# Eleven weight-panel subtractions of a four-layer transformer kernel, moved from VectorE to GpSimd

## The chip, the cores and the metric

The kernel runs on one core of a Trainium2 chip, as one launch. The metric is the device time of that core in microseconds, the median of the runs. The profile gives the span from the first to the last instruction of one execution.

## The reference, cut to what matters

One sequence of 256 tokens, 1024 wide, goes through four layers, all in float32: two of a first kind (four mixers: HGRN2, GLA, MLA, gated delta net, then a gated feed-forward) and two of a second kind. This case is about the second kind:

```python
def hybrid_layer(x, p_i, ...):
    h = rmsnorm(x, g_pre_mix)
    proj = h @ w_in                        # 1024 -> 3404 columns, split in 16 parts
    # a: index scores choose 64 keys of 256 per query, then attention on them
    o_a = dsa_attention(rope(a_q), rope(a_k), a_v, rope(a_iq), rope(a_ik), iw)
    o_b = forgetting_attention(b_q, b_k, b_v, log_sigmoid(b_f + b_forget))
    o_c = differential_attention(rope(c_q), rope(c_k), c_v, lam, ...)
    o_d = sliding_window_sink_attention(rope(d_q), rope(d_k), d_v, sinks)
    x = x + rmsnorm(concat(o_a, o_b, o_c, o_d) @ w_out, g_post_mix)
    m = square(relu(rmsnorm(x, g_pre_mlp) @ w_up)) @ w_down
    x = x + rmsnorm(m, g_post_mlp)
    return x + sigmoid(x @ w_ple_gate) * (p_i @ w_ple_proj)
```

## The kernel before, in words

The 256 tokens are two tiles of 128. The state `x` stays in SBUF, and so do the activations; only weights are streamed. A weight panel is 128 partitions by 2048 float32 values (256 columns of a 1024-row matrix, 1 MB). Panels go through a ring of eight slots, in a fixed list, loaded by SyncE's queue; SyncE waits for the slot to be given back before it issues a load. Layers are named 10, 11 (first kind) and 20, 21 (second kind).

**Split products.** Most matrix products are made in three passes. A float32 matrix is split into a high part, rounded to the format `fp32r`, and a low part, the rest; TensorE then multiplies high by high, high by low and low by high (`mm3`). A panel is split in two steps. ScalarE copies it, rounded, into a second ring slot (`round_weights`, L2577; it increments `rounded`). VectorE then subtracts that copy from the panel in place (`subtract_rounded`, L2760), which gives the low part, and increments `subtracted`. Before it uses a panel TensorE waits until `subtracted` has reached that panel's number (`split_panel`). Both semaphores count the panels of all layers in the order of the list. TensorE alone gives a panel's two slots back.

**A second-kind layer up to its output projection.** Of the fifteen panels of `w_in`, the first four (in3, in4, in5, in9: the index queries, keys and weights, the forget gate) aren't split. The eleven others, here called panels 1 to 11, are, in the order in10, in11, in6, in7, in12, in0, in1, in8, in2, in13, in14; all are 128 x 2048. Four panels of `w_out` follow as 12 to 15. `PANELS` lists these fifteen.

**The order of work.** Every engine runs its instructions in the order in which the program wrote them. Within this part of the layer that order is written by hand: `ORDER` has a list for TensorE, ScalarE and VectorE, and `emit` takes the next piece of the generator that each word names. The word `panel` is one rounding in ScalarE's list and one subtraction in VectorE's; `in` is a projection's piece (TensorE), its copy out of PSUM (ScalarE), its rotation (VectorE: L2797 multiplies the rotated half from PSUM, L2802 the plain half, L2804 adds); `h` is the split of the layer's input; `index` weighs the index scores (L2927, L2929), `select` picks the 64 largest by rounds of `max` and `match_replace` (L2861 to L2870); `a` to `d` are the mixers: masked scores (L2822) and their maximum (L2826), probabilities (L2846 to L2852), later pieces.

**The split of h** (`split_h_in`, L411 to L420) is done for each token tile: two subtractions of 128 x 512, L417 and L419, and then the semaphore `h_split`. It writes over `h`, so it waits until TensorE has made the small unsplit projection of that tile. TensorE waits for both tiles' `h_split` before its first split panel.

**Between engines.** TensorE needs a free PSUM bank for every product (eight banks, given back by the engine that reads them). The masked scores of mixer c take all eight. The transposes of probabilities (L2242) wait for VectorE's `probs`.

GpSimd has no program of its own.

Of the kernel before, what the change touches and what calls it, by code (L numbers as in the profile page):

```python
# [11 lines left out]
ALU = mybir.AluOpType  # L12
# [8 lines left out]
DEPTH = 2  # L21
# [153 lines left out]
class LayerRing:  # L175
# [27 lines left out]
    def rounded_by_act(self, name):  # L203
        return self.ring.rounded, self.ring.split[f"{self.layer}.{name}"] + 1

    def subtracted_by_dve(self, name):
        return self.ring.subtracted, self.ring.split[f"{self.layer}.{name}"] + 1


# [5 lines left out]
class Memory:  # L215
# [12 lines left out]
    def rounded(self, ap):  # L228
        return bass.AP(tensor=self.other[ap.tensor.name], offset=ap.offset, ap=ap.ap)


def as_float32(ap):
    return ap.bitcast(F32)
# [75 lines left out]
class Kit:  # L309
# [156 lines left out]

    def split_panel(self, pe, ring, name):

        pe.wait_ge(*ring.subtracted_by_dve(name))
        return self.rounded(ring.view(name + "_hi")), self.rounded(ring.view(name))  # L470

    def free_panel(self, ring, name):
# [1646 lines left out]
def block2(nc, ctx, kit, banks, ring_all, A, earlier):  # L2119

    rounded, hT, mixT, x = kit.rounded, kit.hT, kit.mixT, kit.x
# [61 lines left out]
    def scores_of(buffer, t, maps):  # L2183
# [35 lines left out]
            c in panel in c b panel c panel b in c panel in forget b c:2 in b c b:2 a panel b in a:2 panel in split a:4  # L2219
            in d p split:2 d a early panel early d:2 early late d:2 early rest d rest d late rest:2"""),  # L2220
        "DVE": in_order("""
            in:2 panel h panel h in:3 panel:3 in:3 index select index panel in panel c:2 select forget:2 c:2 panel
            forget in b in c panel b c in c panel c in panel b:2 c a c b:2 in b panel a panel a b in a split panel in
            a:3 split:2 d in d:2 panel d early p early d a early rest early d:2 rest late rest late d rest"""),
    }
    MIXERS = [(name, t) for name, *_ in ATTENDED for t in range(NT)]
    maxima, probabilities, exponentials = (turns_in(ORDER[engine], {(name, t): (name, first + t) for name, t in MIXERS})
# [518 lines left out]
    def upper_half_in(act, layer, t):  # L2746
        kit.upper_half_of_hT(act, psum_of(layer), "hT0", t, par_of(layer)("pre_mix"))
        kit.round_upper_half(act, t)

    def vector(dve, layer):  # L2750

        psum, ring, due = psum_of(layer), ring_of(layer), due_in(layer)
# [15 lines left out]
            V.tensor_tensor(rounded(lo), a, as_float32(rounded(hi)), ALU.subtract)  # L2768

        def split_panels():  # L2770
            for name in PANELS:
                subtract_rounded(name)
                yield

# [322 lines left out]

    out = Group()
    out.tensor, out.scalar, out.vector, out.load = tensor, scalar, vector, load
    out.transposes_in, out.upper_half_in, out.lower_half_in = transposes_in, upper_half_in, lower_half_in  # L3100
    out.finish_scalar, out.finish_vector = finish_scalar, finish_vector
    out.angles_of, out.rope_tables, out.columns_in = angles_of, rope_tables, small_in
# [6 lines left out]
def two_blocks(nc, A, out):  # L3109

    with ExitStack() as ctx:
# [27 lines left out]
        with nc.Block() as block:  # L3139
# [38 lines left out]
            def _(act):  # L3178
# [7 lines left out]
                for n, (kind, layer) in enumerate(layers):  # L3186
# [18 lines left out]
                    else:  # L3205
                        for _ in ending:
                            pass

            @block.vector
            def _(dve):  # L3210
                dve.wait_ge(ident_in, 16)
                for t in range(NT):
                    kit.scale_rows(dve, 0, t)
                dve.wait_ge(first.columns_in, 16)
                for t in range(NT):
                    first.lower_half_in(dve, 0, t)
                for n, (kind, layer) in enumerate(layers):
                    if (kind, layer) == (first, DEPTH - 1):
                        kind.vector(dve, layer, second.angles_of)
                    else:  # L3220
                        kind.vector(dve, layer)
                    last = n + 1 == len(layers)
                    for _ in kind.finish_vector(dve, layer, 0):
                        pass
                    if not last:
                        after, its = layers[n + 1]
                        kit.scale_rows(dve, 2 * n + 2, 0)
                    ending = kind.finish_vector(dve, layer, 1)
                    next(ending)
                    if not last:  # L3230
                        if after is second and not its:
                            dve.wait_ge(second.columns_in, 16)
                        after.lower_half_in(dve, its, 0)
                    next(ending, None)
                    if not last:
                        kit.scale_rows(dve, 2 * n + 2, 1)
                        after.lower_half_in(dve, its, 1)
# [25 lines left out]
```

## Time and profile before

| What | us |
|---|---|
| median of three runs | 1697.64 |
| lowest and highest | 1693.14, 1698.69 |
| the profiled execution | 1691.87 |
| its span, first to last instruction | 1689.8 |
| TensorE busy | 1594.9 (94%) |
| VectorE busy | 1093.3 (65%) |
| ScalarE busy | 776.6 (46%) |
| GpSimd busy | 0.2 |

The mean granted clock of TensorE is 0.973 of full speed. PE is TensorE's matmuls, PEld its weight loads, DVE is VectorE, ACT ScalarE, POOL GpSimd, SP SyncE; a name with q is an engine's sequencer (a drain or semaphore instruction). L2760 is line 2760 of the kernel. A busy TensorE isn't TensorE at its peak, since matmuls are pipelined and the clock can be granted at half speed. The span was taken on one execution; the idle time of an engine that bounds nothing costs nothing.

### The profile page before, as it was taken

To read this page: it belongs to the slowest core of one execution; us is meant where nothing else is said; L and a number is where in the kernel's file an instruction comes from. 1 tells how busy PE (TensorE), PEld (TensorE's weight loads), DVE (VectorE), ACT (ScalarE), POOL (GpSimd) and SP (SyncE) were. 2 spreads that over 40 slices of the span, in tenths; PEclk is the share of its full clock that TensorE was granted. 3 is DMA by queue.
4 is the path that set the end of the run, shared out by engine and by line. 5 is a ranking of instruction groups with operands and counts; after the bars stand their busy time and mean duration, and the time that the engine had idled before them with its cause. 6 is when DMAs were issued, how large, how long until landed. Compare 5 with 4: busy or idle time off the path is not lost.

```text
span 1689.8 us, 29634 instructions
## 1 busy us (share of the span) xinstructions
PE 1594.9 (94%) x12124; PEld 1425.8 (84%) x12124; DVE 1093.3 (65%) x1609; ACT 776.6 (46%) x1199; POOL 0.2 (0%) x4
## 2 busy tenths in 40 slices
PE   7998988999999989799999989999999979999998
PEld 7987568998898856799989877899889977799887
DVE  3866666776476665577754898666453798666545
ACT  4534254444435332544444455755344346655434
POOL 0000000000000000000000000000000000000000
PEclk9999898999999989899999999999999989999999
DMA  7521033555642200366554433455554432356552
GB/s 247 157 74 52 1 98 118 190 177 202 192 138 68 77 26 7 114 219 198 189 200 120 125 78 104 145 177 203 188 194 133 136 89 100 125 157 205 182 192 100
DMA packets 186310, 232.23 MB, mean 137 GB/s; under 512 B 22560, under 2 KB 161600, under 8 KB 186048
## 3 DMA queue, kind: packets, MB, share of 16 engines
q1 hardware_dynamic: 186176, 230.34, 42.2%
q8 instruction: 96, 1.57, 0.4%
q14 instruction: 38, 0.31, 0.1%
HBM read 229.28 MB, written 1.05 MB: 136 GB/s over the span
## 4 chain that ended last, share of the span: by engine, by line
PE 81%; DVE 10%; ACT 3%; DVEq 3%; issue 2%; DMA 1%; ACTq 0%; SPq 0%
PE banks L435 80%; DVE all_ring_rounded L2760 2%; DVE all_rest L2929 1%; DVE all_work L2864 1%; DMA all_ring<-in_w_ple_gate 1%; DVEq L2863 1%; ACT all_rest L345 1%; DVE all_work L2848 1%; DVE all_ring_rounded L1612 0%; DVE all_work L2826 0%; PE banks L930 0%; DVE all_work L2822 0%; PE banks L2242 0%; DVE x_state L384 0%; ACT all_rest L2581 0%
## 5 line engine op out<-in xcount | busy, mean ns | idle before, releaser
L435 PE MATMUL banks<-all_mix_rounded,all_ring_rounded 128*128 128x256 f32 (+2 forms) x3584 | 670.4, 288 | 20.6 <-DVEq L431 10.9
L435 PEld LDWEIGHTS banks<-all_mix_rounded,all_ring_rounded 128*128 128x128 f32 (+2 forms) x3584 | 569.6, 194 | 30.0 <-DVEq L431 11.9
L435 PE MATMUL banks<-all_work_rounded,all_ring_rounded 128*128 128x256 f32 x1792 | 512.7, 286 | 0.0
L435 PE MATMUL banks<-all_ring_rounded,all_work_rounded 128*128 128x512 f32 (+1 forms) x1856 | 461.9, 377 | 1.8 <-DVEq L2781 1.4
L435 PEld LDWEIGHTS banks<-all_ring_rounded,all_work_rounded 128*128 128x128 f32 x1856 | 347.2, 188 | 67.8 <-issue 2.7
L435 PEld LDWEIGHTS banks<-all_work_rounded,all_ring_rounded 128*128 128x128 f32 x1792 | 348.1, 194 | 1.8 <-issue 1.4
L2760 DVE TENSOR_TENSOR all_ring_rounded<-all_ring,all_ring_rounded 128x2048 fp32r<-128x2048 f32 x104 | 237.7, 2292 | 150.3 <-ACT all_ring_rounded L2577 147.6
L1612 DVE TENSOR_TENSOR all_ring_rounded<-all_ring,all_ring_rounded 128x2048 fp32r<-128x2048 f32 (+2 forms) x96 | 213.6, 2232 | 82.6 <-ACT all_ring_rounded L1369 80.5
L2577 ACT ACTIVATE all_ring_rounded<-all_ring 128x2048 fp32r<-128x2048 f32 x104 | 198.4, 1910 | 117.7 <-DMA all_ring<-in_w_mlp_down 87.3
L1369 ACT ACTIVATE all_ring_rounded<-all_ring 128x2048 fp32r<-128x2048 f32 (+2 forms) x96 | 177.7, 1858 | 112.4 <-DMA all_ring<-in_w_in 54.5
L435 PE MATMUL banks<-all_work 64*64 64x64 f32 (+10 forms) x2084 | 171.5, 271 | 18.2 <-ACTq L1544 6.0
L435 PEld LDWEIGHTS banks<-all_work 64*64 64x64 f32 (+4 forms) x2084 | 123.1, 152 | 47.2 <-issue 24.8
L435 PE MATMUL banks<-all_ring_rounded,all_mix_rounded 128*128 128x256 f32 (+2 forms) x640 | 143.5, 306 | 3.5 <-DVE all_ring_rounded L2760 2.6
L435 PEld LDWEIGHTS banks<-all_ring_rounded,all_mix_rounded 128*128 128x128 f32 x640 | 103.5, 191 | 12.3 <-DVE all_ring_rounded L2760 3.2
L435 PE MATMUL banks<-all_work,all_ring 128*128 128x128 f32 x704 | 100.3, 286 | 1.9 <-issue 1.9
L435 PEld LDWEIGHTS banks<-all_work,all_ring 128*128 128x128 f32 x704 | 86.5, 192 | 2.9 <-issue 2.9
L1586 ACT ACTIVATE all_work<-all_work 128x256 f32<-128x256 f32 x44 | 18.4, 418 | 124.3 <-DVE all_work L2020 124.3
L1373 ACT ACTIVATE all_work<-banks 128x512 f32<-128x512 f32 (+2 forms) x74 | 37.2, 502 | 81.5 <-PE banks L435 65.4
L435 PEld LDWEIGHTS banks<-all_rest,all_work 128*64 128x64 f32 (+2 forms) x504 | 48.4, 164 | 22.8 <-issue 9.0
L435 PE MATMUL banks<-all_rest,all_work 128*128 128x128 f32 (+5 forms) x504 | 60.6, 289 | 6.9 <-ACTq L2582 5.0
L435 PE MATMUL banks<-all_work,all_rest 128*64 128x256 f32 (+7 forms) x292 | 58.6, 379 | 2.1 <-ACT all_work L1380 1.8
L435 PE MATMUL banks<-all_rest,x_state 128*128 128x128 f32 x256 | 37.1, 305 | 24.5 <-DVE all_rest L392 24.5
(257 smaller groups left out, 1244.4 us busy)
## 6 DMA issues: line engine op xcount, KB each, us to landing
all_ring<-in_w_in SPq DMA_DIRECT2D x48, 1024.0 KB, 5.4
all_ring<-in_w_mlp_up SPq DMA_DIRECT2D x32, 1024.0 KB, 5.3
all_ring<-in_w_mlp_down SPq DMA_DIRECT2D x32, 1024.0 KB, 4.9
all_ring<-in_ffn_w_gate SPq DMA_DIRECT2D x22, 1024.0 KB, 5.3
all_ring<-in_ffn_w_up SPq DMA_DIRECT2D x22, 1024.0 KB, 5.4
all_ring<-in_ffn_w_down SPq DMA_DIRECT2D x22, 1024.0 KB, 4.9
all_ring<-in_w_out SPq DMA_DIRECT2D x16, 512.0 KB, 4.2
all_ring<-in_w_out SPq DMA_DIRECT2D x8, 1024.0 KB, 5.0
```

The source lines that it names most:

```text
L345: A_(junk, self.x[:, t, 512 * half:512 * half + 512], ACT.Square, accum_out=s[:, 10 + 4 * half + t:11 + 4 * half + t])
L435: ins = self.nc.tensor.matmul(out, lhsT, rhs, start=start, stop=stop)
L1369: A_(rounded(ring.view(name + "_hi")), raw, ACT.Copy).then_inc(ring_all.rounded, 1)
L1373: A_(out, psum.bank(name)[rows, part], func, scale=scale).then_inc(*psum.freed(name))
L1586: A_(gcv[:, j % 2, 2, :], gcv[:, j % 2, 1, :], ACT.Gelu_apprx_tanh).then_inc(S["ff_gelu"], 1)
L1612: V.tensor_tensor(rounded(ring.view(name)), ring.view(name), as_float32(rounded(ring.view(name + "_hi"))), ALU.subtract).then_inc(ring_all ...
L2577: A_(rounded(ring.view(name + "_hi")), raw, ACT.Copy).then_inc(ring_all.rounded, 1)
L2760: V.tensor_tensor(rounded(ring.view(name)), ring.view(name), as_float32(rounded(ring.view(name + "_hi"))), ALU.subtract).then_inc(ring_all ...
L2848: V.tensor_tensor(L, L, rec.unsqueeze(2).broadcast_to([P, maps, n]), ALU.mult)
L2863: dve.drain()
L2864: V.max(best, acc[t])
L2929: last = V.scalar_tensor_tensor(acc[t], r, weight, acc[t], ALU.mult, ALU.add)
```

## The change

In layers of the second kind GpSimd gets a program, `general`: for each of the layer's eleven split panels of `w_in`, it waits for ScalarE's rounding, subtracts, and increments `subtracted`. Ahead of its first panel in a layer it waits until all earlier panels are counted, so that the counts stay in order. VectorE's list loses eleven of its fifteen `panel` words (and `h panel h` becomes `h:2`), and VectorE waits, before the first of the four that are left (the panels of `w_out`), for the eleventh to be counted. `proj`, `up`, `down` and `ple` panels stay with VectorE, as does everything in layers of the first kind. TensorE's, ScalarE's and SyncE's programs are unchanged.

```diff
--- before.py
+++ after.py
@@ -203,7 +203,7 @@
     def rounded_by_act(self, name):
         return self.ring.rounded, self.ring.split[f"{self.layer}.{name}"] + 1
 
-    def subtracted_by_dve(self, name):
+    def once_subtracted(self, name):
         return self.ring.subtracted, self.ring.split[f"{self.layer}.{name}"] + 1
 
 
@@ -466,7 +466,7 @@
 
     def split_panel(self, pe, ring, name):
 
-        pe.wait_ge(*ring.subtracted_by_dve(name))
+        pe.wait_ge(*ring.once_subtracted(name))
         return self.rounded(ring.view(name + "_hi")), self.rounded(ring.view(name))
 
     def free_panel(self, ring, name):
@@ -2219,9 +2219,9 @@
             c in panel in c b panel c panel b in c panel in forget b c:2 in b c b:2 a panel b in a:2 panel in split a:4
             in d p split:2 d a early panel early d:2 early late d:2 early rest d rest d late rest:2"""),
         "DVE": in_order("""
-            in:2 panel h panel h in:3 panel:3 in:3 index select index panel in panel c:2 select forget:2 c:2 panel
-            forget in b in c panel b c in c panel c in panel b:2 c a c b:2 in b panel a panel a b in a split panel in
-            a:3 split:2 d in d:2 panel d early p early d a early rest early d:2 rest late rest late d rest"""),
+            in:2 h:2 in:6 index select index in c:2 select forget:2 c:2 forget in b in c b c in c:2 in b:2 c a c b:2 in
+            b panel a panel a b in a split panel in a:3 split:2 d in d:2 panel d early p early d a early rest early d:2
+            rest late rest late d rest"""),
     }
     MIXERS = [(name, t) for name, *_ in ATTENDED for t in range(NT)]
     maxima, probabilities, exponentials = (turns_in(ORDER[engine], {(name, t): (name, first + t) for name, t in MIXERS})
@@ -2747,6 +2747,16 @@
         kit.upper_half_of_hT(act, psum_of(layer), "hT0", t, par_of(layer)("pre_mix"))
         kit.round_upper_half(act, t)
 
+    def general(pool, layer):
+
+        ring = ring_of(layer)
+        for n, name in enumerate(PANELS[:-4]):
+            if not n:
+                pool.wait_ge(ring_all.subtracted, ring.rounded_by_act(name)[1] - 1)
+            pool.wait_ge(*ring.rounded_by_act(name))
+            nc.gpsimd.tensor_tensor(rounded(ring.view(name)), ring.view(name), as_float32(rounded(ring.view(name + "_hi"))),
+                                    ALU.subtract).then_inc(ring_all.subtracted, 1)
+
     def vector(dve, layer):
 
         psum, ring, due = psum_of(layer), ring_of(layer), due_in(layer)
@@ -2768,7 +2778,8 @@
             V.tensor_tensor(rounded(lo), a, as_float32(rounded(hi)), ALU.subtract)
 
         def split_panels():
-            for name in PANELS:
+            dve.wait_ge(*ring.once_subtracted(PANELS[-5]))
+            for name in PANELS[-4:]:
                 subtract_rounded(name)
                 yield
 
@@ -3097,6 +3108,7 @@
 
     out = Group()
     out.tensor, out.scalar, out.vector, out.load = tensor, scalar, vector, load
+    out.general = general
     out.transposes_in, out.upper_half_in, out.lower_half_in = transposes_in, upper_half_in, lower_half_in
     out.finish_scalar, out.finish_vector = finish_scalar, finish_vector
     out.angles_of, out.rope_tables, out.columns_in = angles_of, rope_tables, small_in
@@ -3206,6 +3218,11 @@
                         for _ in ending:
                             pass
 
+            @block.gpsimd
+            def _(pool):
+                for layer in range(DEPTH):
+                    second.general(pool, layer)
+
             @block.vector
             def _(dve):
                 dve.wait_ge(ident_in, 16)
```

## Rows read from the trace of the kernel before

**Rows 1.** The page: engines, the chain by engine, VectorE's subtractions in second-kind layers.

```profile
PE 1594.9 (94%) x12124; PEld 1425.8 (84%) x12124; DVE 1093.3 (65%) x1609; ACT 776.6 (46%) x1199; POOL 0.2 (0%) x4
...
PE 81%; DVE 10%; ACT 3%; DVEq 3%; issue 2%; DMA 1%; ACTq 0%; SPq 0%
...
L2760 DVE TENSOR_TENSOR all_ring_rounded<-all_ring,all_ring_rounded 128x2048 fp32r<-128x2048 f32 x104 | 237.7, 2292 | 150.3 <-ACT all_ring_rounded L2577 147.6
```

**Rows 2.** Stretches: length, busy us of PE, PEld, DVE, ACT, POOL; clock; DMA share, GB/s.

```profile
923.50:943.30 19.80, 19.80 (x152) 18.50 (x152) 14.62 (x24) 6.63 (x6) 0.00 (x0) 1.00 0.52 160
...
961.10:966.00 4.90, 1.24 (x6) 0.66 (x4) 4.90 (x5) 0.98 (x2) 0.00 (x0) 0.83 0.00 0
966.00:971.30 5.30, 5.27 (x25) 5.30 (x26) 4.92 (x10) 2.80 (x15) 0.00 (x0) 0.52 0.63 191
...
1001.00:1061.00 60.00, 56.40 (x393) 47.47 (x393) 45.88 (x69) 36.45 (x76) 0.00 (x0) 1.00 0.32 106
...
1360.80:1366.00 5.20, 5.17 (x33) 5.20 (x34) 4.82 (x10) 2.70 (x14) 0.00 (x0) 0.73 0.64 198
```

**Rows 3.** TensorE's timeline, layer 20: start, length, what, [idle before <- who].

```profile
923.49 0.40 PE L435 MATMUL banks<-all_mix_rounded,all_ring_rounded 128*128 128x256 f32 x1
...
929.36 0.38 PE L435 MATMUL banks<-all_work 128*128 128x256 f32 x1
...
966.03 0.55 PE L435 MATMUL banks<-all_mix_rounded,all_ring_rounded 128*128 128x256 f32 x1 [2.77 <-DVE all_work L2822]
...
986.59 1.11 PE L2242 MATMUL banks<-all_rest,all_work 128*128 128x128 f32 x4 [4.49 <-DVEq L2854]
...
993.14 0.51 PE L435 MATMUL banks<-all_ring_rounded,all_mix_rounded 128*128 128x256 f32 x2 [0.17 <-DVE all_ring_rounded L2760]
```

**Rows 4.** TensorE's waits, 1290 to 1457 us: total, times, longest, in us.

```profile
PE banks L2242 <- DVEq L2854: 4.5, 1, 4.5
...
PE banks L435 <- DVE all_work L2822: 2.8, 1, 2.8
```

**Rows 5.** VectorE's timeline, layer 20, in order of time.

```profile
915.94 2.29 DVE L2760 TENSOR_TENSOR all_ring_rounded<-all_ring,all_ring_rounded 128x2048 fp32r<-128x2048 f32 x1 [7.51 <-ACT all_ring_rounded L2577]
...
922.12 0.69 DVE L417 TENSOR_TENSOR all_work_rounded<-all_work,all_mix_rounded 128x512 fp32r<-128x512 f32 x1
922.73 0.68 DVE L419 TENSOR_TENSOR all_work_rounded<-all_work,all_mix_rounded 128x512 fp32r<-128x512 f32 x1
...
937.31 2.29 DVE L2760 TENSOR_TENSOR all_ring_rounded<-all_ring,all_ring_rounded 128x2048 fp32r<-128x2048 f32 x1 [1.30 <-ACT all_ring_rounded L2577]
...
944.65 0.69 DVE L2804 TENSOR_TENSOR all_work<-all_work 128x512 f32<-128x512 f32 x1
...
961.07 4.49 DVE L2760 TENSOR_TENSOR all_ring_rounded<-all_ring,all_ring_rounded 128x2048 fp32r<-128x2048 f32 x2
...
971.13 2.29 DVE L2826 TENSOR_REDUCE all_work<-all_work 128x8 f32<-128x2048 f32 x1
...
973.83 0.43 DVE L2861 TENSOR_TENSOR all_rest<-all_rest,all_work 128x256 f32<-128x256 f32 x1 [0.17 <-issue]
...
983.21 0.43 DVE L2870 TENSOR_TENSOR all_rest<-all_rest,all_work 128x256 f32<-128x256 f32 x1
...
990.80 2.29 DVE L2760 TENSOR_TENSOR all_ring_rounded<-all_ring,all_ring_rounded 128x2048 fp32r<-128x2048 f32 x1
```

**Rows 6.** ScalarE's timeline, layer 20: its roundings of panels.

```profile
913.92 3.71 ACT L2577 ACTIVATE all_ring_rounded<-all_ring 128x2048 fp32r<-128x2048 f32 x2 [0.17 <-issue]
...
919.06 1.91 ACT L2577 ACTIVATE all_ring_rounded<-all_ring 128x2048 fp32r<-128x2048 f32 x1 [0.17 <-DMA all_ring<-in_w_in]
...
941.97 1.91 ACT L2577 ACTIVATE all_ring_rounded<-all_ring 128x2048 fp32r<-128x2048 f32 x1 [4.21 <-DMA all_ring<-in_w_in]
...
971.85 1.91 ACT L2577 ACTIVATE all_ring_rounded<-all_ring 128x2048 fp32r<-128x2048 f32 x1 [0.15 <-issue]
...
980.40 1.91 ACT L2577 ACTIVATE all_ring_rounded<-all_ring 128x2048 fp32r<-128x2048 f32 x1 [0.17 <-issue]
```

## The prediction

> **What bounds the kernel now.** I read the page first. TensorE is busy 94% of the span and carries 81% of the chain that ended last; VectorE carries 10%, and GpSimd ran four tiny instructions in all [rows 1]. So work taken from VectorE brings time only where TensorE waits for VectorE, and the question is where in a second-kind layer that is. The table by stretches of the first such layer (20) gives it [rows 2]. From 923.5 to 943.3 us, where TensorE multiplies split panels, it is busy throughout, and VectorE has idle time. From 961.1 to 966.0 VectorE is full and TensorE nearly empty. From 1001 to 1061 TensorE is at 94%. TensorE's timeline names the two holes [rows 3]: 2.77 us until VectorE's masked scores of mixer c give a bank back, 4.49 us until the probabilities of c are made. Layer 21 (from 1290 us on) has the same two waits [rows 4], so what I work out for layer 20 counts twice.
>
> **What the change removes.** The eleven L2760 subtractions of 2.29 us each leave VectorE in each layer: 22 x 2.29 = 50.4 us of its time [rows 1]. Which of them lie on the path? VectorE's timeline tells [rows 5]. Panels 1 to 5 (from 915.94 to 939.6) stand before 943.3, in a stretch where TensorE is never idle and VectorE is: worth nothing. Without panel 1 the first half of the split of h moves ahead, and nobody waits for it; the second half still needs TensorE's small projection, which ends at 922.1. Panels 6 and 7 are the pair at 961.07 (4.49 us). They stand directly before the masked scores that TensorE waits for, and VectorE has no gap from there to 986.5. This is the only real gain: up to 4.49 us a layer, since the whole chain to the transposes of c moves up. The first hole (2.77 us) is inside that, not beside it, for TensorE then waits longer in the second. Panel 8 (990.80) ends at 993.09, and TensorE's next projection starts at 993.1; before it TensorE had its forget sums, so 0.2 us. Panels 9 to 11 lie after 1000, beside a TensorE that is at 94% [rows 2]: nothing. VectorE's own new wait, for the eleventh panel before its twelfth, has the selection, the scores and probabilities of three mixers ahead of it and costs nothing; neither does GpSimd's first wait, for the layer before. No DMA is moved: a ring slot is given back by TensorE alone, so the loads follow TensorE's time.
>
> **What it adds: eleven instructions on GpSimd.** No row shows GpSimd subtract. Lower end: VectorE's 2.29 us. Upper end: 9.2 us, four such passes. I take 4.6 us: an engine that has to draw the two inputs one after the other needs two passes of 2048 elements, and a pass over 2048 elements with a single input takes VectorE 2.29 us too (the L2826 reduction at 971.13) [rows 5]. The Trainium skill (GPSIMD Engine Reference, section on performance versus the Vector engine) gives 4497 ns for this shape on GpSimd and 2293 ns on VectorE; the trace agrees with the second (2292 ns) and shows nothing of the first, and by 4.5 us the sum would stay within half a microsecond a layer. At 4.6 us GpSimd keeps pace: TensorE takes 5.8 us for a panel of 48 matmuls (923.49 to 929.36) [rows 3], ScalarE's roundings end (start plus length) at 915.8, 917.6, 921.0, then 943.9 (panel 6), 973.8 (8) and 982.3 (9) [rows 6], and panel 1 would be ready at 920.5 against 923.49.
>
> **What GpSimd does to VectorE.** Both read the same memory, and in the trace of before they never run together, so this cost is unknown: nothing at one end, at the other the whole rest of a GpSimd instruction for each VectorE instruction that meets it with two inputs in SBUF. I take the second: the subtraction draws two inputs of 2048 in the 2.29 us that the reduction needs for one [rows 5], so VectorE already reads two streams at full rate there, and the nearest row to a third reader leaves it nothing spare. The first stays in the range. The Trainium skill (SBUF — State Buffer, section on who interferes with whom) says that a VectorE instruction with two SBUF inputs and a GpSimd instruction that reads SBUF lock each other out, the later one for the whole of the earlier; no run here shows it so far, and by it the sum is the one below. The meetings, each by its rows:
> - The split of h, second half (L417 at 922.12, L419 at 922.73) [rows 5]. GpSimd does panel 1 from 915.9 to 920.5 and panel 2 to 925.1, so L417 waits 3.0 us. TensorE's first split matmul is at 923.49, right behind L419 [rows 3]: +3.0 us on the path. If GpSimd's panel 3 gets in between L417 and L419, it is +7.2 (end 930.5 + 0.2).
> - The clock. TensorE, idle for that while, comes back slower: after the 2.77 us hole the granted clock is 0.52 for 5.3 us in layer 20 (about the 1.2 GHz level in place of 2.4) and 0.73 for 5.2 us in layer 21 [rows 2], lost 2.5 and 1.4: +2.0 in the mean. Lower end 0, upper 2.5.
> - Panel 6 (943.9 to 948.5) meets the rotation's sum L2804, wanted at 944.65: +3.9, on VectorE's chain to the scores.
> - Panel 7 is rounded behind VectorE's last index product and meets masked scores, with one input in PSUM, and a reduction: nothing.
> - Panel 8 (973.8 to 978.4) meets L2861 at 973.83, a tie: 0 taken, 4.6 at most. The selection behind it has one input.
> - Panel 9 (982.3 to 986.9) meets L2870, wanted at 983.21: +3.7, directly before the probabilities that TensorE waits for.
> - Panels 10 and 11 come after 1000, where VectorE has also lost three subtractions: nothing.
>
> **The sum.** A layer: +3.0 + 2.0 at the split, then -4.49 + 3.9 + 3.7 = +3.1 up to the transposes of c, together +8.1. Two layers: +16.2. The profiled execution took 1691.87 us (span 1689.8 and 2.1 around it): 1691.9 + 16.2 = 1708.1, say 1708. The median of the three runs is 1697.64, 5.8 us above it; on that footing it would be 1714. What is late next is the transposes of c at 986.59 plus 8.1. This case alone runs from +3 a layer (split delayed, most meetings missed by a microsecond) to +15 (panel 3 gets in first, panel 8 hits): 1698 to 1722.
>
> **Rivals.**
> - No interference. Then -4.5 a layer at the transposes of c and at best another 2.3 for panel 8: -9 to -13.6, 1678 to 1683. For it: VectorE is without a gap exactly where TensorE is idle [rows 2, 5], and panel 6 is rounded at 943.9 [rows 6], 17 us before VectorE comes to it. Against it only that two readers of one memory at full rate would have to be free. It decides if L417 still starts at 922.1. This is the case on the other side of no change, faster by 0.5 to 0.8%.
> - They share instead of locking: VectorE's instructions take about twice as long while they meet. Split +1.4 a layer, L2804 +0.7, L2870 +0.4, against -4.49: -2.0 a layer, -4, 1688. No row speaks for or against it.
> - GpSimd is the bound: TensorE wants panel 3 at 923.5 + 2 x 5.9 = 935.3 [rows 3], and it is ready at 915.9 + 3 x the length, so 6.5 us is the point. At the upper end of 9.2 us it is ready at 943.5, +8.2, and panels 4 and 5 fall behind by 3.3 each, less TensorE's own work for the index between them, some 2: about +13 a layer, 1718.
>
> **How the numbers follow.** A comparison of this kernel can tell about 0.3% (5 us) from no change. Locking as forecast 0.50, no interference 0.28, sharing 0.14, GpSimd as the bound 0.08. Faster by over 0.3%: 0.28 and a third of sharing, 0.32. Within: the rest of sharing and the low edge of my case, 0.09 + 0.08, 0.17. Slower: 0.51. The predicted time is the likeliest case's, 1708. Cases of both signs hold most of the chance, so the range is wide, 1682 to 1723: it reaches from no interference (1683 on the profiled footing, 1689 on the median's) to the upper end of the locking case; the likeliest case's own is 1698 to 1722.
>
> **What would show it.** In the profile after: eleven GpSimd subtractions a layer near 4.6 us from start to start (over 6.5 and the third rival holds); VectorE's busy time lower by some 50 us or, if a blocked instruction is shown as long, lower by less, with L417, L419 and L2804 of some microseconds in place of 0.69; TensorE's first split matmul of layer 20 some 3 us later after the last one of the small projection, a new wait of TensorE on the split of h (L420), and a stretch at a low granted clock behind it; the 2.77 us hole still there; the 4.49 us hole longer. I am wrong if L417 starts within 0.3 us of its small projection's end in both layers and keeps 0.69 us: then the transposes of c come 4.5 us sooner and the kernel is faster. I am wrong in size if VectorE never gets in between two GpSimd instructions.

## The result: slower by 27 us, and the profile after

The kernel after takes 1724.8 us (median of four runs, 1724.0 to 1725.0) against 1697.4 before: a ratio of 1.0165, 95% interval 1.0147 to 1.0183. The direction was right and the size wrong: I had said 1708, with 1723 as the upper end. One execution of the later kernel x5_hold3 took 8719 us where its other three took 1716 to 1724; its cause is not known, and it is left out of that kernel's time and ratio.

The page of the profile after, the lines that answer to [rows 1]:

```profile
PE 1611.2 (94%) x12124; PEld 1438.4 (83%) x12124; DVE 1098.0 (64%) x1587; ACT 776.8 (45%) x1199; POOL 103.3 (6%) x26
...
L2770 DVE TENSOR_TENSOR all_ring_rounded<-all_ring,all_ring_rounded 128x2048 fp32r<-128x2048 f32 x82 | 187.9, 2292 | 132.7 <-ACT all_ring_rounded L2577 130.6
...
L2757 POOL TENSOR_TENSOR all_ring_rounded<-all_ring,all_ring_rounded 128x2048 fp32r<-128x2048 f32 x22 | 103.1, 4698 | 1334.6 <-ACT all_ring_rounded L2577 1334.5
```

The 22 subtractions have left VectorE (104 are now 82), and yet it is busy for longer than before, 1098.0 against 1093.3 us. GpSimd takes 4.70 us for one; I had put 4.6. TensorE's timeline of layer 20, against [rows 3], each with its idle time before:

```profile
932.98 0.58 PE L435 MATMUL banks<-all_mix_rounded,all_ring_rounded 128*128 128x256 f32 x1 [6.75 <-DVEq L420]
```

```profile
973.38 3.21 PE L435 MATMUL banks<-all_work 32*128 32x256 f32 x8 [1.58 <-ACT all_rest L2630]
...
1003.24 1.12 PE L2242 MATMUL banks<-all_rest,all_work 128*128 128x128 f32 x4 [8.39 <-DVEq L2865]
```

(The windows of the timeline are separate queries; the columns are as in [rows 3].) Layer 20 begins 2.46 us later in this execution (VectorE's last small instruction ahead of the layer's split starts at 910.72, before at 908.26), which unchanged layers account for; all delays below are counted from there. So the first split matmul comes 932.98 - 923.49 - 2.46 = 7.0 us late, behind an idle stretch of 6.75, and the transposes of c 1003.24 - 986.59 - 2.46 = 14.2 us late, behind 8.39. The 2.77 us hole before the masked scores of c, which I had said would still be there, is now 1.58 us and ends with ScalarE. Near the end of the mixers the delay is 15.0 us: a matmul of the output projection that stood at 1040.4 now stands at 1057.9. In layer 21 the two marks lie 70.98 us apart, in layer 20 70.26; before it was 63.1 in both. Two layers make 30 of the 33 us between the two profiled spans (1722.9 and 1689.8); the execution shown of before was 5.5 us below the median of 1697.4, hence 27 between medians.

VectorE's timeline of layer 20 tells what fills the time. Line 2760 and all below it have moved by about ten: L2804 is now L2815, L2831 is L2842, L2868 is L2879. Two of these, not shown ahead of the prediction, stood in the kernel before as

```profile
968.27 0.17 DVE L2831 TENSOR_SCALAR all_work<-all_work 128x8 f32<-128x8 f32 x1
...
982.84 0.29 DVE L2868 TENSOR_SCALAR all_rest<-all_rest 128x256 f32<-128x256 f32 x1
```

and in the kernel after VectorE's lines are

```profile
924.51 3.48 DVE L417 TENSOR_TENSOR all_work_rounded<-all_work,all_mix_rounded 128x512 fp32r<-128x512 f32 x1 [11.14 <-PE banks L435]
927.92 4.98 DVE L419 TENSOR_TENSOR all_work_rounded<-all_work,all_mix_rounded 128x512 fp32r<-128x512 f32 x1
...
948.76 4.93 DVE L2815 TENSOR_TENSOR all_work<-all_work 128x512 f32<-128x512 f32 x1
...
955.37 4.92 DVE L2815 TENSOR_TENSOR all_work<-all_work 128x512 f32<-128x512 f32 x1
...
960.56 0.29 DVE L2938 TENSOR_SCALAR all_rest<-all_rest,all_work 128x128 f32<-128x128 f32 x1 [0.19 <-issue]
...
976.02 0.42 DVE L2833 SCALAR_TENSOR_TENSOR all_work<-banks,all_work 128x256 f32<-128x256 f32 x1
...
978.82 2.37 DVE L2842 TENSOR_SCALAR all_work<-all_work 128x8 f32<-128x8 f32 x1
...
986.58 0.43 DVE L2872 TENSOR_TENSOR all_rest<-all_rest,all_work 128x256 f32<-128x256 f32 x1 [0.17 <-issue]
...
995.59 4.19 DVE L2879 TENSOR_SCALAR all_rest<-all_rest 128x256 f32<-128x256 f32 x1
```

and GpSimd's the instructions that they met:

```profile
918.44 13.91 POOL L2757 TENSOR_TENSOR all_ring_rounded<-all_ring,all_ring_rounded 128x2048 fp32r<-128x2048 f32 x3 [918.00 <-ACT all_ring_rounded L2577]
...
948.15 5.00 POOL L2757 TENSOR_TENSOR all_ring_rounded<-all_ring,all_ring_rounded 128x2048 fp32r<-128x2048 f32 x1 [0.44 <-ACT all_ring_rounded L2577]
954.66 5.08 POOL L2757 TENSOR_TENSOR all_ring_rounded<-all_ring,all_ring_rounded 128x2048 fp32r<-128x2048 f32 x1 [1.52 <-ACT all_ring_rounded L2577]
976.62 4.54 POOL L2757 TENSOR_TENSOR all_ring_rounded<-all_ring,all_ring_rounded 128x2048 fp32r<-128x2048 f32 x1 [16.88 <-ACT all_ring_rounded L2577]
986.60 4.90 POOL L2757 TENSOR_TENSOR all_ring_rounded<-all_ring,all_ring_rounded 128x2048 fp32r<-128x2048 f32 x1 [5.43 <-ACT all_ring_rounded L2577]
995.14 4.50 POOL L2757 TENSOR_TENSOR all_ring_rounded<-all_ring,all_ring_rounded 128x2048 fp32r<-128x2048 f32 x1 [3.64 <-ACT all_ring_rounded L2577]
```

Read them in pairs. L417 (0.69 us before) starts at 924.51 and lasts until 928.0, 0.5 us after GpSimd's second panel, whose end the trace has at 927.45. L419 then takes 4.98 us: panel 3, which ends at 932.35, has got in between. The two L2815 end at 953.7 and 960.3, 0.5 us after panels 5 and 6 (the two that start at 948.15 and 954.66). L2842 multiplies eight numbers and takes 2.37 us instead of 0.17, ending with panel 7. L2879 is 4.19 instead of 0.29, ending 0.1 us after panel 9. L2872 stands 0.02 us ahead of panel 8 and is untouched; panel 8 takes 4.90 us.

### The profile page after: what moved, and what is told of

It is laid out like the page before. It is cut to its first block, busy times and chain, and to the rows that moved or that the text cites. A ratio compares the mean times of both kernels' runs of the same rounds, so it can differ in the third digit from the quotient of the medians.

```text
span 1722.9 us, 29640 instructions
## 1 busy us (share of the span) xinstructions
PE 1611.2 (94%) x12124; PEld 1438.4 (83%) x12124; DVE 1098.0 (64%) x1587; ACT 776.8 (45%) x1199; POOL 103.3 (6%) x26
## 4 chain that ended last, share of the span: by engine, by line
PE 79%; DVE 10%; ACT 3%; DVEq 3%; issue 2%; DMA 1%; ACTq 1%; PEld 0%; SPq 0%; PEldq 0%
PE banks L435 78%; DVE all_ring_rounded L2770 1%; DVE all_work L2815 1%; DVE all_rest L2940 1%; DVE all_work L2875 1%; DVEq L420 1%; DMA all_ring<-in_w_ple_gate 1%; DVEq L2874 1%; ACT all_rest L345 1%; DVE all_rest L2879 1%; DVE all_work_rounded L417 0%; ACT all_ring_rounded L1369 0%; PE banks L2242 0%; DVE all_ring_rounded L1612 0%; DVE all_work L2837 0%
## 5 line engine op out<-in xcount | busy, mean ns | idle before, releaser
L2770 DVE TENSOR_TENSOR all_ring_rounded<-all_ring,all_ring_rounded 128x2048 fp32r<-128x2048 f32 x82 | 187.9, 2292 | 132.7 <-ACT all_ring_rounded L2577 130.6
L435 PE MATMUL banks<-all_work 64*64 64x64 f32 (+10 forms) x2084 | 180.1, 274 | 19.6 <-ACTq L1544 6.7
L2757 POOL TENSOR_TENSOR all_ring_rounded<-all_ring,all_ring_rounded 128x2048 fp32r<-128x2048 f32 x22 | 103.1, 4698 | 1334.6 <-ACT all_ring_rounded L2577 1334.5
L435 PEld LDWEIGHTS banks<-all_work 64*64 64x64 f32 (+4 forms) x2084 | 128.3, 154 | 51.4 <-issue 23.5
```

The source lines that it names most:

```text
L435: ins = self.nc.tensor.matmul(out, lhsT, rhs, start=start, stop=stop)
L2757: nc.gpsimd.tensor_tensor(rounded(ring.view(name)), ring.view(name), as_float32(rounded(ring.view(name + "_hi"))), ALU.subtract).then_inc( ...
L2770: V.tensor_tensor(rounded(ring.view(name)), ring.view(name), as_float32(rounded(ring.view(name + "_hi"))), ALU.subtract).then_inc(ring_all ...
```

## The experiments

Four theories had to be told apart. **Lock**: a VectorE instruction that meets GpSimd's waits for the whole of it. **Sharing**: both run, slower. **Pace**: GpSimd's 4.7 us make panels late. **Order**: the new list and waits cost the time. All kernels but the first are the kernel after or before with a small edit; they were compared with the kernel before on the same chip (medians 1694.6 to 1697.0).

### The meeting by itself (m1_meet)

A kernel of its own: `GpSimd: tensor_tensor(p_o, p_a, p_b, subtract)` of 128x2048 starts, VectorE reduces 512 numbers and then issues one instruction under test.

> A small kernel of its own, no part of the transformer: fifteen times VectorE starts GpSimd's subtraction of 128x2048, runs a reduction of 0.7 us and then one instruction under test; afterwards the same instructions run alone. Lock theory: a tensor_tensor with two SBUF inputs (0.69 us alone) lasts until GpSimd's instruction ends, 4 us or more, and so do the immediate-scalar tensor_scalars of 8 and of 512 elements and the copy from SBUF; those with one input in PSUM, the reduction, max and the pointer-scalar tensor_scalar keep their time alone. Sharing theory: the two-input ones take about twice their time alone (1.4 us), the others are untouched. No-interference theory: all keep their time alone. Where GpSimd only writes (fill), lock theory has the two-input subtraction free; where it copies, blocked for the copy.

VectorE's timeline; the part from 89 us on is without GpSimd. Line 66 is the reduction ahead of each case. GpSimd's subtraction lasts 4.50 us and starts with it.

```profile
12.93 4.27 DVE L72 TENSOR_TENSOR o<-a,b 128x512 f32<-128x512 f32 x1
...
18.15 0.69 DVE L73 TENSOR_TENSOR o<-bank,b 128x512 f32<-128x512 f32 x1
...
27.42 4.00 DVE L75 TENSOR_SCALAR o<-a 128x512 f32<-128x512 f32 x1
...
32.37 3.75 DVE L76 TENSOR_SCALAR o<-a 128x8 f32<-128x8 f32 x1
...
37.07 4.01 DVE L77 TENSOR_SCALAR o<-a 128x512 f32<-128x512 f32 x1
...
51.67 0.69 DVE L80 TENSOR_REDUCE junk<-a 128x1 f32<-128x512 f32 x1
...
56.30 0.43 DVE L81 MAX8 junk<-a 128x8 f32<-128x256 f32 x1
...
61.34 3.60 DVE L82 COPY o<-a 128x512 f32<-128x512 f32 x1 [0.49 <-issue]
...
65.89 0.69 DVE L83 COPY o<-bank 128x512 f32<-128x512 f32 x1
...
79.93 0.69 DVE L86 TENSOR_TENSOR o<-a,b 128x512 f32<-128x512 f32 x1
...
89.14 0.69 DVE L72 TENSOR_TENSOR o<-a,b 128x512 f32<-128x512 f32 x1
...
91.44 0.43 DVE L75 TENSOR_SCALAR o<-a 128x512 f32<-128x512 f32 x1
91.94 0.17 DVE L76 TENSOR_SCALAR o<-a 128x8 f32<-128x8 f32 x1
92.19 0.49 DVE L77 TENSOR_SCALAR o<-a 128x512 f32<-128x512 f32 x1
```

Two inputs in SBUF: 4.27 us in place of 0.69. One of them in PSUM (L73): 0.69. An immediate tensor_scalar (L75, L76) and one with a pointer scalar (L77, and L78 with 3.75 us) of 512 or of 8 numbers, one of 511 (L79, 4.00) and a copy from SBUF (L82) are all held until GpSimd is done. The reduction, max and the copy from PSUM are not. With GpSimd only filling (L86, 79.93) the two-input subtraction keeps 0.69. The lock theory holds in each case but one: I had expected the pointer-scalar form to be free. Sharing falls: none of the held 512-number or 8-number instructions took merely twice as long, and each ended within 0.6 us of GpSimd's end. The Trainium skill (SBUF — State Buffer, section on who interferes with whom) names copies and tensor_scalars in a two-port mode among those that contend, and a GpSimd instruction that only writes as harmless to two inputs. These rows agree: the held one-input forms of 512 numbers take 0.43 to 0.49 us alone where the reduction takes 0.69, which fits such a mode without proving it.

### Nobody subtracts (x1_none)

```diff
-            nc.gpsimd.tensor_tensor(rounded(ring.view(name)), ring.view(name), ...).then_inc(ring_all.subtracted, 1)
+            pool.sem_inc(ring_all.subtracted, 1)
```

(Not shown: TensorE multiplies the rounded panel where it took the low part.)

> In layers of the second kind nobody subtracts the eleven panels; GpSimd only counts them when they are rounded, and TensorE takes the rounded panel in place of the low part (the low part of these weights is left out; the matmuls are as many). Lock theory: what the change takes from VectorE is then a pure gain, 4.5 to 6.8 us a layer, 1684 to 1688 against a before of 1697. A theory by which the new order of VectorE's list or the waits cost the time: still slower than before, above 1710.

1685.5 us, ratio 0.9944 (0.9928 to 0.9961): 5.0 us a layer faster by the medians. The order theory falls, and the gain of -4.49 a layer is right: the trace has the transposes of c 58.7 us behind the first split matmul (983.10 and 924.36), 63.1 before, so 4.4 us are gained there. The 0.2 us of panel 8 don't show.

### Panels 1 to 5 alone, and 6 to 11 alone (x2_first5, x3_last6)

```diff
-        for n, name in enumerate(PANELS[:-4]):
+        for n, name in enumerate(PANELS):
+            if n + 1 not in ON_POOL:      # {1..5}, or {6..11}
+                continue
```

(VectorE keeps the other panels at their places, and each side waits for the other's last count.)

> GpSimd subtracts only panels 1 to 5 of a layer, VectorE 6 to 15 at their places of before. Lock theory: the split of h is blocked as in the changed kernel (TensorE idle 6.7 us before its first split matmul), one rotation too, and nothing is gained: 8 to 11 us a layer, 1713 to 1719. Pace theory (GpSimd's 4.7 us make panels late): nearly the whole loss of 27 us here too, since panels 1 to 5 are the ones used soonest, and TensorE's waits are on the count of panels, not on the split of h.

> GpSimd subtracts only panels 6 to 11, VectorE 1 to 5 and 12 to 15. Lock theory: the split of h is as before; 4.5 us a layer gained by panels 6 and 7, about 4 lost at a rotation of c, 2 at the small tensor_scalar after the masked scores, 4 at the tensor_scalar that ends the second selection: +5 to +6 a layer, 1707 to 1710. Pace theory: within 3 us of before. No interference from single-input instructions (my prediction's assumption): the last two do not show and the loss is at the two-input addition after the selection.

1714.9 us, ratio 1.0116 (1.0097 to 1.0134), and 1708.1, ratio 1.0081 (1.0064 to 1.0097), each inside what was expected. The waits of TensorE that grew most in the two (in us: total, times, longest):

```profile
PE banks L435 <- DVEq L420: 16.4, 4, 6.7
```

```profile
PE banks L2240 <- DVEq L2868: 16.6, 2, 8.4
```

The loss of the first five is at the split of h, 6.7 us at most. The loss of the last six is before the transposes of c, where the wait is 8.4 us at most and 4.5 before (L2240 stands for L2242 there). In neither does a matmul wait for GpSimd (one weight load of x3_last6 waits 0.2 us): the pace theory falls. The parts add to 1.97% against 1.65 together, a difference about as large as the three intervals allow; in the traces the delays of the two layers add to 30.7 us for the parts and are 29.6 together, so there is nothing left to explain beyond about a microsecond.

### Holding GpSimd back at the split (x4_hold, x5_hold3)

```diff
+            if n == 1:                     # x5_hold3: if n == 2
+                pool.wait_ge(kit.sems["h_split"], NT * split_event(layer))
             pool.wait_ge(*ring.rounded_by_act(name))
```

> The changed kernel with one more wait: GpSimd starts a layer's panel 2, and all behind it, only when VectorE has split h. Lock theory: L417 and L419 take 0.69 us each again, TensorE's idle 6.7 us before the first split matmul is gone in both layers, and what is left is the loss of the run with panels 6 to 11: 1707 to 1711. If it was the later start of the panels that cost, this is slower than the changed kernel.

> The same wait, but before panel 3: panel 2 still meets L417, and nothing can get in between L417 and L419. This is the case that my prediction took as likely. L417 waits for the end of panel 2 (3.5 us long), L419 takes 0.69 us, TensorE is idle 2.4 to 3.0 us in place of 6.7; some 4 us a layer less than the changed kernel, 1715 to 1718. If VectorE and GpSimd took turns whatever is queued, it would be equal to the changed kernel.

Both expectations on the time missed: 1726.8 (1.0189, 1.0173 to 1.0204) and 1719.8 us (1.0145, 1.0124 to 1.0167), neither clear of the kernel after. What they say of the instructions was right: in x4_hold L417 and L419 take 0.69 again, in x5_hold3 L417 3.48 and L419 0.68, and TensorE's idle time there is 0 and 2.4. But look at x4_hold's timelines:

```profile
920.96 0.69 DVE L417 TENSOR_TENSOR all_work_rounded<-all_work,all_mix_rounded 128x512 fp32r<-128x512 f32 x1 [11.14 <-PE banks L435]
921.57 0.68 DVE L419 TENSOR_TENSOR all_work_rounded<-all_work,all_mix_rounded 128x512 fp32r<-128x512 f32 x1
...
922.98 4.54 DVE L2815 TENSOR_TENSOR all_work<-all_work 128x512 f32<-128x512 f32 x1
927.62 4.83 DVE L2817 TENSOR_TENSOR all_work<-all_work 128x512 f32<-128x512 f32 x1
```

```profile
935.30 1.19 PE L435 MATMUL banks<-all_work 128*128 128x256 f32 x2 [6.88 <-DVE all_work L2895]
```

Panels 2 and 3, held until 922.4, now meet the two instructions of the first rotation that have both inputs in SBUF, the multiplication L2815 (L2802 before) and the addition L2817 (L2804 before), 4.54 and 4.83 us. TensorE then waits 6.88 us, until 935.30, for a PSUM bank that VectorE empties behind them. The stall has moved, not gone. In x5_hold3 the held panel 3 meets the same multiplication,

```profile
932.37 4.51 DVE L2815 TENSOR_TENSOR all_work<-all_work 128x512 f32<-128x512 f32 x1
```

and of the 4.3 us saved at L419 2.5 are left at the transposes of c in layer 20 and 1.7 in layer 21. So my picture of a VectorE with slack from 923.5 to 943.3 was too kind: the kernel before has VectorE busy for 14.6 of these 19.8 us, with gaps of 1.3 to 1.6 us, and a blocked instruction adds about 4.

### GpSimd writes but does not read (x6_write_only)

```diff
-            nc.gpsimd.tensor_tensor(rounded(ring.view(name)), ring.view(name), ..., ALU.subtract)
+            nc.gpsimd.memset(ring.view(name), 0.0)
```

> GpSimd fills each of the eleven panels with zeros in place of subtracting, at the same places and with the same counts, and TensorE takes the rounded panel for the low part (the low parts of these weights are left out). GpSimd then writes and does not read. The small kernel showed the fill beside a two-input subtraction with neither longer (0.69 us). Lock on the read side: L417, L419 and L2815 take 0.69 us, 1685 to 1690, as with no subtraction at all. A cost of semaphores or of mere GpSimd activity: above 1710.

1688.9 us, ratio 0.9962 (0.9948 to 0.9975). (TensorE takes the rounded panel for the low part, as in x1_none.) With 22 GpSimd instructions and all the semaphores of the change in place the kernel is faster than before; L417 and L419 stand at 0.69 and 0.68. The fills last 1.8 us, so a shorter stay is part of it too; the small kernel has the two-input case free beside a fill. But a fill isn't harmless to every form. The tensor_scalar at the end of the second selection, 0.29 us before, meets one and ends 0.1 us after it, in both layers:

```profile
981.76 1.49 DVE L2879 TENSOR_SCALAR all_rest<-all_rest 128x256 f32<-128x256 f32 x1
```

```profile
981.30 1.80 POOL L2758 MEMSET all_ring<- 128x2048 f32 x1 [6.73 <-ACT all_ring_rounded L2578]
```

### One term at a time (y1_p23, y2_p6, y3_p7, y4_p9, y5_p89)

The same edit as in x2_first5 with `ON_POOL` {2, 3}, {6}, {7}, {9} and {8, 9}.

> GpSimd subtracts panels 2 and 3 of a second-kind layer alone. If the split of h is a term of its own: L417 3.5 us, L419 5.0, TensorE idle 6.7 us before the first split matmul, nothing gained, 6.7 to 9 us a layer (the idle and up to 2 us of low clock), 1709 to 1713 against 1695.5. If it is only part of a loss that the later stretches would make anyway: under 1705.

> GpSimd subtracts panel 6 alone, as soon as it is rounded. The addition L2815 of one rotation of c waits for it, +4.2 us; one subtraction of 2.3 us leaves the same chain: +1.9 a layer, 1699. With the same panel inside the first selection (together with panel 8) it was 3.8 us faster than before, so the sign hangs on where it starts.

> GpSimd subtracts panel 7 alone. It meets the masked scores, which have an input in PSUM, and then the multiplication of 8 numbers (L2831 of the kernel before, 0.17 us): +2.2 us, and 2.3 us of subtraction leave the chain: no change, 1694 to 1697. If single-input instructions were free, as my prediction had it: -2.3 a layer, 1691.

> GpSimd subtracts panel 9 alone. It meets the end of the second selection: the tensor_scalar with one input (L2868 of the kernel before, 0.29 us) lasts 4.2 us, directly before the probabilities that TensorE waits for; the subtraction that leaves VectorE lay beside TensorE's work. +3.9 a layer, 1703.

> GpSimd subtracts panels 8 and 9, so that 9 need not wait for VectorE's count of 8. Panel 8 runs beside the second selection and meets nothing long; panel 9 starts some 2 us before the selection's end, and its tensor_scalar with a single input lasts about 4.2 us in place of 0.29. If single-input instructions in SBUF are blocked in the kernel as in the small kernel: +3.9 a layer, 1700 to 1704. If the loss seen there in the changed kernel has another source: within 2 us of before.

| kernel | us | ratio, interval | a layer |
|---|---|---|---|
| y1_p23 | 1712.9 | 1.0101 (1.0085, 1.0118) | +8.6 |
| y2_p6 | 1701.7 | 1.0033 (1.0022, 1.0044) | +2.8 |
| y3_p7 | 1694.8 | 0.9998 (0.9986, 1.0009) | 0 |
| y4_p9 | 1695.0 | 0.9993 (0.9981, 1.0005) | -0.6 |
| y5_p89 | 1702.2 | 1.0043 (1.0028, 1.0058) | +3.6 |

(The last column is half of the ratio's excess times the median of before.) Three came out as said: the split is a term of its own (y1_p23), panel 7's gain and block are nearly equal (y3_p7), and with panel 8 beside it panel 9 makes the end of the selection last 4.2 us (y5_p89). In y1_p23 it is the first token tile's pair that is held (L417 5.06, L419 4.98 us), since GpSimd starts there only when VectorE has counted panel 1, and TensorE is idle for 6.1 us. In y2_p6 the sign is right and the size short: +1.9 a layer was expected, the trace has +2.7 (the block 4.2, the removed subtraction worth 1.6). Panel 9 alone missed: 1703 expected, no loss. Its row and that of y5_p89 tell why:

```profile
995.82 4.60 POOL L2757 TENSOR_TENSOR all_ring_rounded<-all_ring,all_ring_rounded 128x2048 fp32r<-128x2048 f32 x1 [995.38 <-DVE all_ring_rounded L2770]
```

```profile
983.50 4.50 POOL L2757 TENSOR_TENSOR all_ring_rounded<-all_ring,all_ring_rounded 128x2048 fp32r<-128x2048 f32 x1 [3.63 <-ACT all_ring_rounded L2575]
```

```profile
983.94 4.21 DVE L2882 TENSOR_SCALAR all_rest<-all_rest 128x256 f32<-128x256 f32 x1
```

Alone, panel 9 must wait for VectorE to count panel 8 (the release shown is L2770), starts after the probabilities of c and meets additions from PSUM. With panel 8 on GpSimd too it starts at once, and the single-input L2882 takes 4.21 us. The same GpSimd instruction costs 4 us or nothing by 10 us of its start. So y4_p9 by itself says nothing of the end of the selection; y5_p89 does.

### GpSimd only inside the selections (x8_select, z1_select67)

```diff
+            pool.wait_ge(selecting, 2 * layer + (1 if n == 5 else 2))
             pool.wait_ge(*ring.rounded_by_act(name))
...
-            V.tensor_tensor(acc[t], acc[t], shaped(C("causal"), NT, T)[:, t, 0:n], ALU.add)
+            V.tensor_tensor(acc[t], acc[t], shaped(C("causal"), NT, T)[:, t, 0:n], ALU.add).then_inc(selecting, 1)
```

with `ON_POOL` {6, 8} and {6, 7}; the first of the two panels waits for the first selection, the second for the second.

> A version that puts GpSimd where it meets nothing: it subtracts only panels 6 and 8, the first from the start of the first selection on, the second from the start of the second, since max and match_replace run beside it; all others stay with VectorE at their places of before. Both selections last longer (6.8 and 8.5 us) than its 4.5 us. Lock theory: no VectorE instruction is longer than before, the chain to the transposes of c is 2.3 us shorter, a layer gains 2.3 to 3, the kernel 4.6 to 6: 0.3% faster than before. If the selections' instructions are blocked after all: 4 us a layer slower.

> GpSimd subtracts panel 6 from the start of the first selection on and panel 7 from the start of the second. VectorE's chain to the transposes of c loses both subtractions, 4.5 us, and meets nothing. But TensorE is done with panel 6's product some 4 us before panel 7 is ready, so the gain is taken back in part: 1689 to 1692, like the version with panels 6 and 8 (1691.7). If TensorE has slack there: 1687.

x8_select: 1691.7 us, ratio 0.9979 (0.9970 to 0.9988); z1_select67: 1687.0, ratio 0.9952 (0.9937 to 0.9967). Both beat the kernel before, which itself beats the change, and both do all of the work. x8_select gained 3.8 us where I had expected 4.6 to 6, z1_select67 gained 7.6 where I had expected 3 to 6, with 1687 us named for the case that TensorE has slack. In z1_select67 TensorE does wait for panel 7, and still wins:

```profile
972.37 4.53 POOL L2759 TENSOR_TENSOR all_ring_rounded<-all_ring,all_ring_rounded 128x2048 fp32r<-128x2048 f32 x1 [15.96 <-DVE all_rest L2877]
```

```profile
976.95 0.53 PE L435 MATMUL banks<-all_mix_rounded,all_ring_rounded 128*128 128x256 f32 x1 [3.84 <-POOL all_ring_rounded L2759]
...
991.26 0.50 PE L435 MATMUL banks<-all_ring_rounded,all_mix_rounded 128*128 128x256 f32 x2 [1.33 <-DVE all_ring_rounded L2772]
```

The 3.84 us at 976.95 replace the wait for the probabilities: the transposes of c, 63.1 us behind the first split matmul before, are at 985.92, 60.0 behind the one at 925.91, without a wait. By the medians the version keeps 7.6 of the 10.0 us that x1_none shows as the most that these eleven can give; the two intervals overlap, and in the traces both have the output projection of layer 20 4.3 us earlier.

## Why the prediction was right and wrong

**What bounds it, and the gain.** Right. The two holes were the places, and -4.49 us a layer was the gain (x1_none: 4.4 at the transposes of layer 20, 5.0 a layer by the medians). I had added 0.2 for panel 8, which no trace shows; what panels 1 to 5 and 9 to 11 give is too small to see there.

**GpSimd's price.** Right: 4.6 forecast, 4.50 in m1_meet, 4.70 in the mean of the kernel after. The rival by which it would be the bound did not come; no matmul waited for a panel of it, and one weight load did for 0.2 us.

**The whole wait at a meeting.** Right, and now shown: 4.27 us for 0.69 in m1_meet. Of the rivals, no interference and sharing both fall with that row.

**The split of h.** This is the first step that failed. I took +3.0 and named +7.2 as the case in which GpSimd's panel 3 gets in between L417 and L419. It does, in both layers: +7.0 in the kernel after, L419 at 4.98; x5_hold3, where panel 3 can't be queued, has L419 at 0.68. I had no reason for taking +3.0. L417 did get its turn between panels 2 and 3; while it ran, panel 3 stood ready and L419 was only the next of VectorE, and panel 3 went first. 4.0 us a layer.

**Instructions with one input.** The second. I wrote that panel 7 meets nothing and that the selection behind panel 8 has one input, as if one input were free. Max and match_replace are, a tensor_scalar isn't. It cost 2.2 us at L2842 (panel 7), where I had put nothing. The 3.7 that I had put on L2870, a two-input addition, fell on the tensor_scalar in front of it with 3.9: the number came out by luck.

**Panel 6 at the rotation.** +3.9 forecast; the addition took 4.2 more in y2_p6 and in the kernel after. There panel 5 met the addition of the other rotation of c too, which I hadn't listed. It cost nothing: VectorE, rid of its subtractions, had come to it 3 us sooner than TensorE's delay of 8.3, and waits for TensorE before the second rotation; in x2_first5, where panel 5 alone meets a rotation, the delay stays what it was. The index work begins 960.56 - 945.61 - 2.46 = 12.5 us late, of which 7.0 are the split, 1.2 the clock and 4.2 this block. That panels 1 to 5 can do no harm beyond the split still doesn't hold in general: in x4_hold, where panels 2 and 3 start later, they stall TensorE for 6.9 us.

**The clock.** +2.0 a layer forecast. It is there, smaller. Granted clock by stretches of the kernel after, an idle time and what follows it, then around the transposes:

```profile
926.20:933.00 6.80, 0.05 (x2) 0.03 (x1) 6.69 (x2) 0.00 (x0) 6.15 (x2) 0.71 0.00 0
933.00:938.00 5.00, 5.00 (x31) 5.00 (x32) 4.50 (x12) 0.39 (x1) 0.00 (x0) 0.72 0.66 202
...
976.00:980.00 4.00, 3.51 (x10) 2.08 (x9) 3.83 (x7) 1.03 (x2) 3.38 (x1) 0.50 0.01 4
...
1003.20:1009.00 5.80, 5.76 (x27) 5.76 (x28) 4.84 (x8) 0.60 (x1) 0.00 (x0) 0.50 0.01 3
```

Behind the split the granted clock is 0.72 in the mean of 5 us, between the two levels, and behind the later holes 0.50, the 1.2 GHz level. The former makes TensorE another 1.2 us late in layer 20 (VectorE's first multiplication from the next split product, L2797 at 930.06 before, is L2808 at 940.77: 8.3 us late against 7.0) and 1.9 in layer 21, and it stays in the chain, since VectorE's rotations wait for these products. In y1_p23, where only the split is hit, the transposes of c come 2.3 us later than the first split matmul alone would make them (8.7 against 6.35): the term by itself, as forecast.

**The sum.** Forecast 8.1 a layer. In layer 20 the steps measured are +7.0 at the split (3.0 forecast), +1.2 for the clock (2.0), +4.2 for panel 6 at the rotation (3.9), -4.4 for the two subtractions (L2833 starts 976.02 - 965.47 - 2.46 = 8.1 us late, -4.49 forecast), +2.2 for panel 7 (0) and +3.9 for panel 9 (3.7): 14.1, and the trace has 14.2 at the transposes. It has 15.0 at the output projection. TensorE is already 14.8 late 7 us behind the transposes (993.14 before, 1010.41 after), ahead of two more instructions that are held (L2842 by 1.4 at 1021.26, L2813 by 3.6 at 1023.64), so these can add 0.2 at most; what makes the 0.6 before them no run here separates. The lock was right; the steps that failed were the turn of panel 3 (4.0) and the tensor_scalar that meets panel 7 (2.2). They make 6.2 us a layer, and the sum fell short by 6.1 at the transposes, since the smaller errors nearly cancel. A further part of the distance to 1708 is footing: I had added to the profiled execution, and the forecast itself has 1714 on the median's.

## What to carry to other kernels

Before moving elementwise work from VectorE to an idle GpSimd, list for each of its instructions what VectorE issues while it runs, here in the next 4 to 5 us. Two SBUF inputs, and copies or tensor_scalars within SBUF however small, were held to its end in every meeting of these traces but one, in which both engines started within the same hundredth of a microsecond (x5_hold3, 955.12); an input in PSUM, a reduction, max and match_replace were not. What is moved is worth its place, not its length: two panels a layer started where VectorE selects gave 7.6 us, eleven a layer started as soon as possible cost 27. And if GpSimd has its next instruction ready, count it in between two VectorE instructions of a kind that is held, even if they follow each other directly.

## What the hardware did that I had not expected

- A tensor_scalar of eight numbers is held as long as one of 512: 3.75 us for 0.17 (m1_meet, L76), with a pointer scalar too, 3.75 for 0.23 (L78).
- The two engines took turns: when VectorE's held instruction had run, GpSimd's queued one went before VectorE's next. L419 waited for all of panel 3 (4.98 us) right after L417 had waited for panel 2; L2815 and L2817 in x4_hold did the same (4.54, 4.83).
- GpSimd's own instructions hardly suffer: 4.50 us in m1_meet, 4.50 to 5.08 in the kernel after.
- A GpSimd copy of 128x2048 takes 1.89 us and holds a two-input VectorE instruction for what is left of it (1.65 for 0.69, L85); a fill takes 1.80 and doesn't hold that (0.69, L86), but in x6_write_only a fill held a tensor_scalar (L2879, 1.49 for 0.29).
